# Two blocks on one core: the first product behind each norm in two sweeps of tokens (three chunks, then the last), output products chunk by chunk, PSUM banks taken one by one

## What is computed

```python
def first_block(x, ...):
    for layer in range(2):
        h = rms_norm(x, norm_mix_g[layer])
        x = x + (mixer_ab(h, ...) if layer % 2 == 0 else mixer_rglru(h, ...))
        h = rms_norm(x, norm_ffn_g[layer])
        x = x + hierarchical_moe(h, ...)         # 32 experts, top 2 in the top group
    return rms_norm(x, norm_final_g)

def second_block(x, ...):
    for i in range(2):
        h = rmsnorm(x, ln1_g[i]) @ w_in[i]       # fox, diff and mla heads
        x = x + concat([fox, diff, mla]) @ w_o[i]
        up = causal_dwconv(rmsnorm(x, ln2_g[i]) @ w_up[i], conv_w[i], conv_b[i])
        x = x + (silu(up[..., :2816]) * up[..., 2816:]) @ w_down[i]
    return rmsnorm(x, final_g)
```

## Time and profile before

| | |
|---|---|
| median of 3 runs | 2879.21 us (2877.5 to 2879.88) |
| profiled execution, its own time | 2876.93 us |
| its span | 2875.7 us |
| PE busy | 2737.2 us (95%), 14944 matmuls |
| PEld busy | 1894.1 us (66%) |
| DVE, ACT, POOL busy | 1221.8, 910.1, 367.7 us |
| mean granted TensorE clock | 0.959 |

### The profile page before, as it was taken

How to read it: one execution, slowest core, us unless ns; L and a number is a source line. 1 busy time by engine, 2 the same in 40 slices (tenths; PEclk the granted TensorE clock), 3 DMA queues, 4 the chain that set the end, 5 groups by cost and what they waited for, 6 DMA issues and landing times. The chain is left out here.

```text
span 2875.7 us, 36485 instructions
## 1 busy us (share of the span) xinstructions
PE 2737.2 (95%) x14944; PEld 1894.1 (66%) x14944; DVE 1221.8 (42%) x2275; ACT 910.1 (32%) x1666; POOL 367.7 (13%) x197
## 2 busy tenths in 40 slices
PE   7989999999878999999979999999999999999998
PEld 5865455444757545544467767788887776788887
DVE  1542223223755222322246652552553674356254
ACT  4331101111473111111154543442344454343233
POOL 3200000000330000000030011222222001122122
PEclk9989999999988999999999978999999996899999
DMA  5147999998315799999722011223232101123312
GB/s 203 61 188 314 406 402 407 397 406 340 103 44 200 310 406 406 400 402 406 320 85 74 30 59 44 88 88 106 71 109 68 65 17 57 54 79 102 104 59 81
DMA packets 134825, 543.60 MB, mean 189 GB/s; under 512 B 14592, under 2 KB 26112, under 8 KB 85376
## 3 DMA queue, kind: packets, MB, share of 16 engines
q1 hardware_dynamic: 127120, 536.94, 48.4%
q10 hardware_dynamic: 7536, 4.28, 0.5%
HBM read 539.09 MB, written 2.10 MB: 188 GB/s over the span
## 5 line engine op out<-in xcount | busy, mean ns | idle before, releaser
L500 PE MATMUL ps<-w,w 128*128 128x512 f32 x3360 | 769.7, 391 | 19.2 <-POOL w L256 10.1
L500 PEld LDWEIGHTS ps<-w,w 128*128 128x128 f32 x3360 | 632.5, 188 | 153.7 <-DVE w L443 9.8
L256 POOL TENSOR_TENSOR w<-w,w 128x1024 fp32r<-128x1024 f32 (+3 forms) x139 | 339.0, 2450 | 2267.1 <-ACT w L248 2267.1
L502 PE MATMUL ps<-w,w 128*128 128x512 f32 (+2 forms) x2256 | 495.5, 381 | 24.5 <-DVE w L981 15.2
L502 PEld LDWEIGHTS ps<-w,w 128*128 128x128 f32 x2256 | 415.4, 190 | 102.5 <-ACT w L572 15.6
L1185 PE MATMUL ps<-w,w 128*64 128x512 f32 x2048 | 451.6, 594 | 1.8 <-issue 1.8
L248 ACT ACTIVATE w<-w 128x1024 fp32r<-128x1024 f32 (+3 forms) x260 | 251.4, 1000 | 428.0 <-PE ps L500 221.5
L256 DVE TENSOR_TENSOR w<-w,w 128x1024 fp32r<-128x1024 f32 (+3 forms) x121 | 195.2, 1619 | 403.3 <-ACT w L248 400.8
L1185 PEld LDWEIGHTS ps<-w,w 128*64 128x64 f32 x2048 | 146.0, 137 | 285.5 <-issue 285.5
L1410 DVE TENSOR_TENSOR X<-ps,X 128x512 f32<-128x512 f32 x256 | 163.9, 682 | 221.5 <-PE ps L1221 220.5
L1207 PE MATMUL ps<-w,w 128*64 128x512 f32 x1024 | 226.8, 595 | 0.8 <-ACT w L1262 0.8
(11 more groups left out here) (234 smaller groups left out, 2305.4 us busy)
## 6 DMA issues: line engine op xcount, KB each, us to landing
w<-in_moe_w_gate SPq DMA_DIRECT2D x128, 1024.0 KB, 10.2
w<-in_moe_w_up SPq DMA_DIRECT2D x128, 1024.0 KB, 12.9
w<-in_moe_w_down SPq DMA_DIRECT2D x128, 1024.0 KB, 8.1
w<-in_w_up SPq DMA_DIRECT2D x40, 1024.0 KB, 5.1
w<-in_w_down SPq DMA_DIRECT2D x20, 1024.0 KB, 5.1
w<-in_w_in SPq DMA_DIRECT2D x16, 1024.0 KB, 5.1
w<-in_ab_w_in SPq DMA_DIRECT2D x10, 1024.0 KB, 5.1
w<-in_c_w_in SPq DMA_DIRECT2D x8, 1024.0 KB, 5.9
```

The lines of the kernel that those rows point to most:

```text
L256: up(self.wlo[self.low[s][0]], lane.e.tensor_tensor(lo, raw, hi.bitcast(F32), ALU.subtract))
L500: ins = pe.matmul(bank[:, :], wp[:, k, P * o:P * o + P], ap(k0 + k), start=first, stop=stop)
L502: ins = pe.matmul(bank[:, 0:width], ap(k0 + k)[:, P * o:P * o + P], wp[:, k, :], start=first, stop=stop)
```

## The change

- `TAIL` becomes 4: the output products of the mixers and the attention (second half of the columns) run wholly chunk by chunk.
- `tensor_product` takes each bank at its first use, in place of all four ahead.
- `tensor_norm_features` goes. `tensor_first_product` takes its place and that of the stage's first `tensor_product`: it transposes chunks 0 to 2 of six blocks, runs the product over k for the first 384 tokens, transposes blocks 6 and 7 after k = 0 and the last chunk (two further banks) after k = 2, and then runs the last 128 tokens, out by out over all k. Its weight halves are all held to its end.
- In attention and FFN, chunks 0 and 1 of six blocks are transposed ahead of the last chunk's matmuls in the previous output product (`ahead`). The root and norm of the last chunk move behind the fourth block of the features.
- At the start, only two weight halves are converted ahead of the features.

```diff
-TAIL = 2
+TAIL = 4
+HEAD = P * (NT - 1)
...
+    def scalar_norm_features(gain, last_square, late):
+        late = list(late)
         for k in range(KD):
-            vector_feature(HTH[:, k, :], HTL[:, k, :], gain(k))
+            bank = bf.next(S)
+            up(fhi, act.activation(HTH[:, k, 0:HEAD], bank[:, 0:HEAD], ACT.Identity, scale=gain(k)))
+            if k == 3 and last_square:
+                last_square()
+            if k in (5, 7) and late:
+                W.hi(late.pop(0))
+        for k in range(KD):
+            if k % 4 == 0:
+                bank = bl.next(S)
+            up(lhi, act.activation(HTH[:, k, HEAD:T], bank[:, P * (k % 4):P * (k % 4) + P], ACT.Identity, scale=gain(k)))
+        for h in late:
+            W.hi(h)
...
+    def tensor_rows_ahead(rows):
+        for k in range(6):
+            tensor_turn_rows(rows, k, (0, 1))
...
+    def tensor_first_product(rows, key, n, width, kind, feature=False):
+        turned = len(rows.banks)
+        for k in range(6):
+            tensor_turn_rows(rows, k, (NT - 2,) if turned else range(NT - 1))
...
+                for o, t in parts:
+                    for pi in range(3):
+                        i = matmul(o, t, weights[k][pi == 2], k, H[pi == 1], k == 0 and pi == 0, k == KD - 1 and pi == 2)
...
+                if k == 0:
+                    for later in (6, 7):
+                        tensor_turn_rows(rows, later, range(NT - 1))
+                if k == 2:
+                    tensor_turn_last_rows(rows)
+        PE.wait_ge(bl.free, 2)
+        for o, t in last:
+            for k in range(KD):
+                for pi in range(3):
+                    i = matmul(o, t, weights[k][pi == 2], k, H[pi == 1], k == 0 and pi == 0, k == KD - 1 and pi == 2)
+            m = up(kind.full, i)
+        for s, _, _ in steps:
+            W.consumed_at[s] = (kind.full, m)
...
-            for o, bank in zip(outs, bs):
+            for o in outs:
+                if o == outs[-1] and ahead:
+                    ahead()
...
         for c in range(NT):
             vector_add_chunk(1, c)
             if c:
                 vector_norm(apply, ((c - 1, 1),))
-        vector_norm(apply, ((NT - 1, 1),))
+        if chunks == NT:
+            vector_norm(apply, ((NT - 1, 1),))
+        return lambda: vector_norm(apply, ((NT - 1, 1),))
```

More of the change, by code:

```diff
@@ L458, in scalar_norm_features, with tensor_turn_rows @@
[L458 to L462, removed]
+    def tensor_turn_rows(rows, k, chunks):
+        if k not in rows.banks:
+            rows.banks[k] = banks.take(bf)
+        for c in chunks:
+            PE.wait_total(xn, rows.before + c + 1)
+            i = pe.transpose(rows.banks[k][:, P * c:P * c + P], rows.XN[:, c, P * k:P * k + P], ident)
+            if c == NT - 2:
+                up(bf.full, i)
@@ new lines, in tensor_rows_ahead, with tensor_turn_last_rows, matmul @@
+    def tensor_rows_ahead(rows):
+        for k in range(6):
+            tensor_turn_rows(rows, k, (0, 1))
+    def tensor_turn_last_rows(rows):
+        for k in range(KD):
+            if k % 4 == 0:
+                bank = banks.take(bl)
+            PE.wait_total(xn, rows.before + NT + k // 4)
+            i = pe.transpose(bank[:, P * (k % 4):P * (k % 4) + P], rows.XN[:, NT - 1, P * k:P * k + P], ident)
+            if k % 4 == 3:
+                up(bl.full, i)
+    def tensor_first_product(rows, key, n, width, kind, feature=False):
+        turned = len(rows.banks)
+        for k in range(6):
+            tensor_turn_rows(rows, k, (NT - 2,) if turned else range(NT - 1))
+        bs = {}
+        def matmul(o, t, w, k, a, first, stop):
+            at_ = o if feature else t
+            if at_ not in bs:
+                bs[at_] = banks.take(kind)
+            if feature:
+                return pe.matmul(bs[o][:, t], w[:, P * o:P * o + P], a(k)[:, t], start=first, stop=stop)
+            return pe.matmul(bs[t][:, 0:width], a(k)[:, P * t:P * t + P], w, start=first, stop=stop)
+        parts = [(o, slice(0, HEAD)) for o in range(n)] if feature else [(0, t) for t in range(NT - 1)]
+        last = [(o, slice(HEAD, T)) for o in range(n)] if feature else [(0, NT - 1)]
+        steps = W.steps(key)
+        weights = []
+        for s, nk, _ in steps:
+            hi, lo = (x.rearrange("p (k n) -> p k n", k=nk) for x in W.need(s, PE))
+            for j in range(nk):
+                k = len(weights)
+                weights.append((hi[:, j, :], lo[:, j, :]))
+                PE.wait_ge(bf.free, k + 1)
+                for o, t in parts:
+                    for pi in range(3):
+                        i = matmul(o, t, weights[k][pi == 2], k, H[pi == 1], k == 0 and pi == 0, k == KD - 1 and pi == 2)
+                    if k == KD - 1 and not feature:
+                        up(kind.full, i)
+                if k == 0:
[5 more added lines that the diff above has]
+        for o, t in last:
+            for k in range(KD):
+                for pi in range(3):
[3 more added lines that the diff above has]
+            W.consumed_at[s] = (kind.full, m)
@@ L480, in program, with tensor_product, bank_of @@
     H = (features_hi, features_lo)
-    def tensor_product(key, outs, width, a, kind, ready, feature=False, between=None, tail=0):
-        bs = [banks.take(kind) for _ in outs]
+    def tensor_product(key, outs, width, a, kind, ready, feature=False, between=None, tail=0, ahead=None):
+        bs = {}
+        def bank_of(o):
+            if o not in bs:
+                bs[o] = banks.take(kind)
+            return bs[o]
         k0 = 0
```

201 lines of the change are left out of this document (112 added, 89 removed).

## The result

The changed kernel took 2941.72 us (median of 4 runs, 2940.52 to 2943.01) against 2878.94 us before (4 runs, 2877.5 to 2879.88): ratio 1.0219, 95% interval 1.0201 to 1.0236. It is 62.8 us slower; 2943 had been predicted. The profiled execution took 2940.52 us, with a span of 2939.3 us and a mean granted clock of 0.953 (before: 0.959).

What follows compares the result with a forecast made beforehand. PE was taken as the bound, busy 2737.2 of 2875.7 us. Terms of +55.9 us, with the clock +64.4, on 2876.93 gave 2941.3; with the median 2.3 above, 2943 was forecast, range 2889 to 2967.

Steps and rivals of the forecast that it cites:

- the clock's term: Lower granted clock behind four new gaps and two stuttering FFN stretches: +8.5 us, between 0 and 14.
- The stall behind the first product: Second product waits for bank copy-outs: +3.9 us in ab and rglru, +3.8 in each attention, +13.8 in each FFN.
- E: The moment at which PE is through with a piece; waits at the seams are counted from it.
- Both halves of my reason: Second product's first bank is the first product's; its copy-out queues behind weight halves held to that product's end.
- The two sweeps: First products of ab, rglru and both FFNs, 384 then 128 columns: +5.8 us each, between +1.0 and +16.7; attention +0.
- Rivals 1 and 2: 128-column matmuls take 0.065 us (2924 us, chance 0.12), or 0.229 us, no cheaper than 512 columns (2987 us, chance 0.05).
- Seams with transposes ahead: At FFN 0, FFN 1 and attention 1, 3.0 and 3.5 us, together 6.5 against 8.36: -1.9 us each.
- The start and rglru: First products start earlier: ab near 20.7 in place of 26.04 (-5.3 us), rglru 736.6 in place of 741.36 (-4.8).
- Waits for normed rows: Sign in the profile after: transposes' waits for normed rows fall from 32.5 to about 20 us, not vanish.
- Block 7's bank: In FFN seams block 7 takes block 4's bank, whose features stand behind the last chunk's norm: about +1.2 us each.
- Rival 3: No stall behind the first product, because copy-outs start during the second sweep: 2892 us, chance 0.11.
- Rival 4: Faster: the last chunk's chain lies beside matmuls, neither loads nor banks make PE wait: 2870 us, chance 0.04.

Runs made afterwards that it cites:

- skip4: The changed kernel with the bank ring moved on by four (three in attention) behind each first product: 2890.98 us.
- copyfirst: The changed kernel with ACT and DVE copying the first product's banks out before they turn to the weight halves: 2892.55 us.
- samebanks: lazy with the ring set back by four behind each of the six first products, so the second product takes the first's banks: 2883.47 us.
- held: samebanks with each weight half of the first product counted as read only at the product's end: 2919.85 us.
- narrow64: The changed kernel with the last sweep of the FFNs' first products at 64 columns in place of 128: 2951.2 us.
- lazy: The kernel before with one part of the change alone, each bank taken at its first use: 2863.73 us.
- noahead: skip4 without the transposes ahead of the last chunk's matmuls in three seams: 2876.2 us.

## Why the prediction was right, point by point

The direction, the size and the mechanism held: 2943 predicted, 2941.7 measured. That the total came within 2 us is in part luck: the clock's term had the right size in the sum, but not in the place where it was lost.

- **The stall behind the first product** (3.9, 3.9, 3.8, 3.8, 13.8, 13.8: 43.0 us). The first waits are 3.65 to 3.67 us in the four small seams (14.7 in 4) and 7.29 + 1.26 + 1.32 + 1.32 = 11.2 in each FFN: 37.1 us of idle time. In the FFN the prediction had the four banks at 6.85, 9.8, 12.8 and 15.8 us behind E; PE began in them at 7.3, 10.2, 13.1 and 16.1. The idle time stays under the term of 13.8 because the three matmuls in each bank took 1.6 us at the low clock and filled more of the 2.97 us. In the small seams the term was idle time alone and came out 0.2 us too large each. Four runs bear on the cause: skip4 and copyfirst take it away from either side, samebanks and held build it up in the kernel before. Both halves of my reason are needed: the ring without the hold costs 20 us (samebanks), the hold on top of it another 36 (held), and the hold without the ring leaves no bank wait (skip4).
- **The two sweeps** (+5.8 a product; 0.174 and 0.115 us a matmul). Measured: 43.3 / 384 = 0.113 for 128 columns, and for 384 columns the starts of matmuls stand 0.173 us apart at the full clock. narrow64 shows that the 4-column row was the right neighbour: from 128 columns down to 64 the time does not fall. Rivals 1 and 2 fall with it. The Trainium skill's figure of about 81 ns ("TensorE: Matmul & The Clock Gate", section "Back-to-back issue gap") isn't met for this pair: here it is 113.
- **Seams with transposes ahead** (3.0 + 3.5 us). Measured 3.0 and 3.7. The sum was right and its reading incomplete: I booked -1.9 us to the whole of the edit. lazy has the same seam at 6.3 without any transposes ahead, and noahead shows them to cost 3.1 us at this seam.
- **The start and rglru** (first product at 20.7 and 736.6). The rows of PE in the changed kernel's timeline:

```profile
20.30 3.47 PE L528 MATMUL ps<-w,w 128*128 128x384 f32 x12 [3.10 <-POOL w L264]
...
54.71 5.55 PE L604 MATMUL ps<-w,w 128*128 128x512 f32 x15 [3.67 <-ACT w L678]
...
741.59 2.34 PE L528 MATMUL ps<-w,w 128*128 128x384 f32 x12
...
1471.52 2.11 PE L529 MATMUL ps<-w,w 128*128 128x416 f32 x9
```

  ab begins at 20.30. For rglru, the forecast of 736.6 and the 4.9 us by which ab's terms move it are 741.5, measured 741.59; for attention 0, 1460.0 and 11.3 us of terms ahead of it are 1471.3, measured 1471.52. Some errors cancel in these sums: ab's input stage alone came out 1.0 us over its terms.
- **Waits for normed rows: missed.** I had them fall from 32.5 to about 20 us; they rose to 37.1, in 13 places in place of 10. What failed is the list of what would show it, not a term of the sum: the two waits of 1.53 and 1.65 us that I had written into the seams' 3.0 and 3.5 are both of this row, against one of 1.43 before, and I didn't add them up.
- **Block 7's bank** (+1.2 in the FFNs). The wait at FFN 1 was 0.57 us: half.
- **The clock** (+8.5). The terms without it came to 55.9 us, the stages to 63.6: 7.7 are left. They lie in the fourth stage above all (6.9), and there the time at 0.5 grew most. `held` shows the same without sweeps: its fourth stage is 24.1 us longer than `lazy`'s, where the stall's terms are 13.8 + 3.8 = 17.6, and has 27.3 us more at 0.5. So the stall's clock loss fits, and the term had spread it over all six seams; no run varies the clock alone.
- **Rival 3** (no stall) had its conditions in copyfirst, and its price: 2892 there, 2892.55 measured. **Rival 4** (faster than before) needed cheap narrow matmuls too, and these don't exist here: skip4, without any stall, is still slower than before.

Where the change lost, then: 50.7 us to the stall and its clock; some 12 to the sweeps in the feature products; 15 to the transposes ahead. Where it gained: 15 by the banks one by one. These are differences between kernels, each with other parts around it; that they nearly add up to 62.8 proves nothing, since the earlier starts at ab, rglru and attention 0 aren't among them.

## What to carry to other kernels

When a product reads its weights twice, ask what waits for them to come free: here ACT's next halves did, and the copy-outs that free the banks stood behind those in its program. Count the banks that a new function takes around the ring, and make sure that the next product's first one isn't the last product's. An edit that fills a wait must be set against the edit that removes it: the norm written directly behind its addition took 20 us off skip4, while the transposes moved ahead cost 15, and the kernel with the small edits alone runs at 0.989 of the time before.

## What the runs showed of the hardware

- An fp32r matmul with its own 128 x 128 weight block takes 0.11 us at the full clock for 128 columns as for 64 (starts 0.111 us apart in the changed kernel, 0.112 in narrow64, medians), near the 0.115 of a 4-column fp32 one. At 384 columns it is 0.173 us.
- In the sweep of 64 columns the granted clock went from 1.00 to 0.50 while PE was never idle, and the starts of matmuls went from 0.112 to 0.213 us apart; the time at 0.5 rose from 277.7 (changed kernel) to 301.2 us. I had expected such a fall behind idle time alone.
- In the stall the clock was low, and it still was when the last bank was there, from 2581.2 to 2598.3 us. A window of it in the changed kernel:

```profile
2582.00:2597.00 15.00, 8.03 (x16) 4.98 (x17) 7.38 (x9) 6.27 (x9) 1.88 (x2) 0.50 0.22 70
```

  Three matmuls took 1.6 us there, and 0.94 and 0.97 in the first two rows of samebanks, which lie at the full clock.
